# v projected ahead of w_conf_out, and triangular levels that keep only X^T: a hybrid conformer / gated-delta / MoE step on one core

## The reference, cut to what matters

```
p   = rmsnorm(h) @ w_in                              # u pair, q, k, v, z, a, b, two gates
c   = silu(layernorm(dwconv31(u)));  y_a = c @ w_conf_out + b_conf_out
qkv = silu(dwconv4(p[q, k, v]));  q, k = l2norm(q), l2norm(k)
a_mat = I + strict_lower(beta k k^T * decay)         # per head and chunk
u, w  = solve(a_mat, [beta v, beta k exp(gc)])       # triangular solve
v_new = u - w S;  o = q_dec S + (q k^T * decay) v_new;  S = S exp(gl) + k_dec^T v_new
h  += (sig(gA) * y_a + sig(gB) * (norm(o) * silu(z)) @ w_dn_out) @ w_out
h  += moe_top4_of_32(rmsnorm(h));   y = rmsnorm(h)
```

## Time and profile before

| what | value |
|---|---|
| median of 3 runs | 1618.7 us (1615.04 to 1619.51) |
| profiled execution | 1620.38 us, span 1618.5 us, mean granted TensorE clock 0.92 |
| busy over the span | PE 81%, PEld 44%, DVE 34%, POOL 14%, ACT 12% |
| HBM traffic | 480.5 MB, mean 297 GB/s |

### The profile page before, as it was taken

One profiled execution on the slowest core, in us unless ns is written; L12 is line 12 of the kernel. 1 busy time (PEld: TensorE's weight loads), 2 busy tenths in 40 slices (PEclk: granted clock), 3 DMA queues, 4 the chain that ended last, 5 costly groups with the idle time before them and its releaser, 6 DMA issues.

```text
span 1618.5 us, 31060 instructions
## 1 busy us (share of the span) xinstructions
PE 1317.7 (81%) x11104; PEld 711.4 (44%) x11105; DVE 542.4 (34%) x1370; ACT 202.0 (12%) x524; POOL 225.8 (14%) x350
## 2 busy tenths in 40 slices
PE   4899999988878987866999896966696987866955
PEld 4677777757867642322343332322232332222312
DVE  2799846175366234101211111111021121101254
ACT  2211232322122020000000000000000000000001
POOL 2006600207131001000100000000010000001310
PEclk9999999998989988887999998988898998888987
DMA  7766545304005678999997999999999999999996
GB/s 140 241 159 119 123 107 154 104 6 114 2 1 178 217 265 350 418 418 416 420 418 289 355 417 419 419 416 420 419 416 420 419 392 391 420 418 418 417 403 240
DMA packets 184543, 480.50 MB, mean 297 GB/s; under 512 B 15932, under 2 KB 113468, under 8 KB 151659
## 3 DMA queue, kind: packets, MB, share of 16 engines
q1 hardware_dynamic: 172909, 463.37, 76.0%
q0 software_dynamic: 2560, 10.29, 1.6%
q10 hardware_dynamic: 9024, 6.17, 1.2%
HBM read 462.42 MB, written 18.21 MB: 297 GB/s over the span
## 4 chain that ended last, share of the span: by engine, by line
PE 61%; DMA 18%; DVE 8%; SPq 6%; issue 4%; ACT 2%; POOL 1%; DVEq 0%; POOLq 0%; ACTq 0%
PE bank L1226 18%; DMA arena<-in_w_up 16%; PE bank L776 15%; PE bank L1238 11%; PE bank L1194 4%; PE bank L1212 3%; SPq L374 2%; PE bank L1118 2%; PE bank L1126 2%; DMA arena<-in_w_in 2%; SPq L442 2%; ACT gate L1621 1%; DVE arena L1955 1%; DVE gate L2226 1%; PE bank L1037 1%
## 5 line engine op out<-in xcount | busy, mean ns | idle before, releaser
L1226 PE MATMUL bank<-arena,gate 128*32 128x512 f32 x3264 | 415.8, 640 | 134.5 <-DMA arena<-in_w_up 134.5
L1226 PEld LDWEIGHTS bank<-arena,gate 128*32 128x32 f32 x3264 | 103.6, 113 | 404.5 <-issue 275.5
L776 PE MATMUL bank<-arena 128*128 128x304 f32 (+1 forms) x1024 | 261.3, 418 | 5.8 <-DMA arena<-in_w_in 4.7
L2241 DVE COPY gate<-bank 128x256 f32<-128x256 f32 x46 | 19.5, 425 | 637.1 <-PE bank L1238 637.1
L776 PEld LDWEIGHTS bank<-arena 128*128 128x128 f32 x1024 | 196.3, 192 | 69.5 <-issue 7.3
L1238 PE MATMUL bank<-arena,gate 128*32 128x256 f32 x3264 | 189.3, 384 | 29.4 <-ACT gate L1621 29.4
L1238 PEld LDWEIGHTS bank<-arena,gate 128*32 128x32 f32 x3264 | 112.5, 111 | 93.9 <-issue 26.6
L1744 DVE SCALAR_TENSOR_TENSOR acc<-arena,pcol,acc x240 | 126.4, 607 | 0.1
L675 POOL TENSOR_TENSOR qkv<-qkv 128x192 f32<-128x192 f32 x46 | 29.3, 638 | 617.7 <-DVE qkv L2185 617.7
L1212 PE MATMUL bank<-qkv 128*128 128x512 f32 x102 | 62.2, 694 | 49.6 <-DVE gate L2227 22.5
L1194 PE MATMUL bank<-qkv 128*32 128x256 f32 (+1 forms) x1224 | 87.8, 403 | 0.7 <-DVE qkv L2149 0.7
(11 more groups left out here) (411 smaller groups left out, 1202.8 us busy)
## 6 DMA issues: line engine op xcount, KB each, us to landing
arena<-in_w_up SPq DMA_DIRECT2D x256, 1024.0 KB, 12.5
arena<-in_w_down SPq DMA_DIRECT2D x256, 512.0 KB, 8.8
arena<-in_w_in SPq DMA_DIRECT2D x64, 512.0 KB, 11.9
y_d<-gate ACTq DMA_DIRECT2D x188, 32.0 KB, 4.9
y_d<-zs POOLq DMA_DIRECT2D x1, 4608.0 KB, 22.2
arena<-in_w_conf_out SPq DMA_DIRECT2D x8, 512.0 KB, 4.9
arena<-in_state_dn_S SPq DMA_DIRECT2D x8, 512.0 KB, 7.2
arena<-in_w_dn_out SPq DMA_DIRECT2D x1, 4096.0 KB, 13.9
```

Source lines behind the costliest of these rows:

```text
L776: last = mm(bank[2 * (j % 2) + f][:, 0:cols.stop - cols.start], wring[:, j, k, P * f:P * (f + 1)], rhs[:, k, cols], start=(k == 0), stop=( ...
L1226: last = mm(hidden(q)[v], xgT[:, i, SL * q0:SL * (q0 + 1)], parts(wup[k], q)[v], start=False, stop=(k == KC - 1), skip_group_check=True)
```

## The change

- v is round 7, and TensorE's l2 sums stand behind its steps. w_conf_out is loaded as round 8 and is applied in eight halves of 128 output columns (`conf_half`, one bank), placed by hand between the setup steps of chunk 0; VectorE evacuates each (`conf_evac`).
- The conf tails are transposed and stored before rounds 5 and 6. The q/k/v tails are turned by plain matmuls with the identity into four 32-partition strips of two banks, copied by two instructions and stored by 12 transfers.
- In a level the two products become one: X^T is kept, X is made of it by transposes and a copy on ScalarE. The last level updates X. X is not built in the setup.
- The constants of the packed work are made before the squares of q and k; token masks, sums, products, start and packed levels move to earlier levels; sample products go to levels 4, 5, 6 and behind k times S.
- Buffers are moved so that the lifetimes allow it: the sample states take the slots of the weight ring (their load waits for the last conf half), `w_out` the chunk buffers (its load waits for `s_done`), the experts' slots follow.

```diff
@@ sync
-            win_group(7, 0, a["w_conf_out"][0].rearrange("(k p) n -> p k n", p=P))
-            win_group(8, 4 * D)
...
+            sp.wait_ge(s["tail_evac"], 2)
             sp.dma_start(a["cp"][0, 0], uout[0:CH, :]).then_inc(s["tail_out"], 16)
...
+            win_group(7, 4 * D)
+            win_group(8, 0, a["w_conf_out"][0].rearrange("(k p) n -> p k n", p=P))
+
+            sp.wait_ge(s["tail_evac"], 4)
+            for b, q in ((0, 0), (0, 1), (0, 2), (0, 3), (1, 0), (1, 1)):
+                cols = slice(2048 * b + 512 * q, 2048 * b + 512 * (q + 1))
+                sp.dma_start(a["dp"][0, 0][:, cols], qout[32 * q:32 * q + SH, b, :]).then_inc(s["qkv_tail_out"], 16)
...
+            sp.wait_ge(s["job_done"], 13 + KC)
             for h in range(H):
                 sp.dma_start(s0[:, h, :, :], a["state_dn_S"][0, :, h].rearrange("n k v -> k n v")
@@ tensor
+            pe.wait_ge(s["ab_ready"], 1)
+            for g in range(2):
+                for k in range(4 * g, 4 * g + 4):
+                    last = nc.tensor.transpose(bank[6 + g][0:62, P * (k % 4):P * (k % 4 + 1)], utail[:, k, :], ident[:])
+                last.then_inc(s["tail_t_done"], 1)
             with pe.Fori(5, 7) as it:
                 win_round(it)
...
+                pe.wait_ge(s["win_bank_free"], 7 * WRING + (j + 1))
+                win_step(7, j, xnT)
+                l2_sums(j)
+
+            def turn_tails():
+
+                pe.wait_ge(s["win_bank_free"], 34)
+                for k in range(24):
+                    b, r = divmod(k, 16)
+                    q, i = divmod(r, 4)
+                    last = mm(bank[5 + b][32 * q:32 * (q + 1), P * i:P * (i + 1)], qtail[:, k, :], ident[:], start=True, stop=True,
+                              skip_group_check=True)
...
+            def conf_half(m):
+
+                j, f = divmod(m, 2)
+                if f == 0:
+                    pe.wait_ge(win_in[j], 8 * 32 + 32)
+                if m:
+                    pe.wait_ge(s["conf_mm_evac"], m)
...
+                for k in range(KC):
+                    last = mm(bank[7][:, 0:N2], wring[:, j, k, P * f:P * (f + 1)], acc[:, k, TS],
+                              start=(k == 0), stop=(k == KC - 1))
+                last.then_inc(s["job_done"], 1)
@@ tensor, chunk 0 setup (rows, then)
+                    conf_half(0)
+                    turn_tails()
+                    conf_half(1)
+                    packed_sums()
+                    conf_half(2)
+                    pe.wait_ge(s["packed_dve"], DVE_STEP["sums"])
+                    pe.wait_ge(s["tail_evac"], 4)
+                    pe.wait_ge(s["l2_scaled"], 16)
... (products k k^T, k q^T)
+                    conf_half(3)
+                    conf_half(4)
... (transposes of k and v)
+                    conf_half(5)
... (transposes of um)
+                    conf_half(6)
+                    packed_rows()
+                    conf_half(7)
@@ tensor, a level
                         for h in range(4 * g, 4 * g + 4):
+                            last = nc.tensor.transpose(bank[2 + g][:, P * (h % 4):P * (h % 4 + 1)], xt[:, h, :], ident[:])
+                        last.then_inc(s["xt_turned"], 1)
+                        for h in range(4 * g, 4 * g + 4):
                             last = mm(bank[g][:, P * (h % 4):P * (h % 4 + 1)], um[:, h, :], xt[:, h, :],
...
+                            left, right = (x, zt) if lev < LEVELS - 1 else (zt, x)
+                            last = mm(bank[g][:, P * (h % 4):P * (h % 4 + 1)], left[:, h, :], right[:, h, :],
                                       start=True, stop=True)
-                        if lev < LEVELS - 1:
-                            for h in range(4 * g, 4 * g + 4):
-                                last = mm(bank[g][:, P * (h % 4):P * (h % 4 + 1)], x[:, h, :], zt[:, h, :],
-                                          start=True, stop=True)
@@ tensor, chunk 0, behind a level's product
+                        if lev == 1:
+                            packed_products()
+                        elif lev == 2:
                             packed_turn()
-                        elif lev == 6:
...
+                        elif lev < 6:
+                            packed_v(lev - 2)
+                            if lev > 3:
+                                sample_products(kmask, "kmask", 0, lev - 4)
+                        else:
+                            meta_state()
                             sample_products(qmask, "qmask", 256, 0)
@@ scalar, a level
+                        act.wait_ge(s["xt_turned"], lev * 2 + (12 * c + g - 1))
+                        fn(heads(u_x, P)[:, 4 * g:4 * g + 4, :], bank[2 + g][:, :].rearrange("p (h n) -> p h n", h=4), ACT.Copy
+                           ).then_inc(s["zt_copied"], 1)
@@ vector, chunk 0 setup
+                    conf_evac(0)
+                    tails_out()
+                    conf_evac(1)
+                    packed_sums()
+                    l2_scale(1)
+                    l2_scale(0)
+                    conf_evac(2)
+                    dve.wait_ge(s["l2_scaled"], 16)
...
-                dve.wait_ge(s["um_ready"], 7 * c + 1)
-                v.tensor_tensor(x, eye.to_broadcast((P, H, P)), um, ALU.subtract)
@@ vector, a level
-                        last = v.tensor_tensor(x[:, hs, :], x[:, hs, :], four(bank[2 + g]), ALU.subtract)
-                        if lev < LEVELS - 1:
-                            last = v.tensor_tensor(xt[:, hs, :], xt[:, hs, :], four(bank[g]), ALU.subtract)
-                        last.then_inc(s["x_updated"], 1)
+                        w = xt if lev < LEVELS - 1 else x
+                        v.tensor_tensor(w[:, hs, :], w[:, hs, :], four(bank[g]), ALU.subtract).then_inc(s["x_updated"], 1)
@@ gpsimd, chunk 0
+                if c == 0:
+                    pool.wait_ge(s["qkv_tail_out"], 16 * 12)
+                    token_masks(kmask, k_p[:, 1:3, :].rearrange("p g n -> p (g n)"), H)
...
                         if lev == 1:
-                            packed_constants()
+                            token_masks(qmask[:, 0:4], q_p[:, 0, :], 4)
...
+                            packed_level(0)
                         elif lev == 3:
-                            packed_sums()
...
+                            token_masks(qmask[:, 4:8], q_p[:, 1, :], 4)
+                            packed_level(1)
+                        elif lev < 6:
+                            packed_level(lev - 2)
```

More of the change, by code:

```diff
@@ L66 @@
 WRING = 4
-STEPS = 9 * WRING
 A_UH = WRING * 2048
@@ L86, in steps @@
     return {name: i + 1 for i, name in enumerate(names.split())}
[L89 removed]
+PE_STEP = steps("spread sums rows u qk ktr vtr umtr zt1 v1 zt2 v2 zt3 v3 ks vnm sm qs vns os ot")
 DVE_STEP = steps("gb sums dt_arg dt uu qk kd x0 x1 x2 x3 vmm s r o scaled out")
 ACT_STEP = steps("packed exps dt vb zt1 zt2 zt3 oq vns root")
[L92 removed]
+POOL_STEP = steps("const um kmask qmask0 um0 qmask um1 um2 um3 vm0 vm1")
 def first(b):
@@ L867, in packed_sums, with packed_rows @@
                 packed(mm(bank[4][:, 68:70], same_s, gb_p[:, 0, 1:3], start=True, stop=True))
+            def packed_rows():
                 pe.wait_ge(s["packed_pool"], POOL_STEP["um"])
-                packed(mm(bank[5][:, 0:384], ones[:], um_p, start=True, stop=True))
+                pe.wait_ge(s["uq_evac"], 8)
+                packed(mm(bank[6][:, 0:384], ones[:], um_p, start=True, stop=True))
             def packed_products():
-                pe.wait_ge(s["packed_dve"], DVE_STEP["sums"])
+                pe.wait_ge(s["packed_dve"], DVE_STEP["dt_arg"])
                 pe.wait_ge(s["packed_act"], ACT_STEP["exps"])
+                pe.wait_ge(s["conf_mm_evac"], KC)
                 for i in range(3):
@@ L925, in meta_state @@
                     rows = slice(32 * r, 32 * (r + 1))
-                    last = mm(bank[2 + r][:, 0:2 * P], kd_p[rows, 0, :], vmeta[rows, :, :], start=True, stop=True)
+                    last = mm(meta_bank[r][:, 0:2 * P], kd_p[rows, 0, :], vmeta[rows, :, :], start=True, stop=True)
                 packed(last)
@@ L1793, in _ @@
             stt(g_t, g_t, -1.0, alog.unsqueeze(1).to_broadcast((P, 3, H)), ALU.mult, ALU.mult).then_inc(s["rates_ready"], 1)
+            for g in range(2):
+                dve.wait_ge(s["tail_t_done"], g + 1)
+                v.tensor_copy(uout[:, 512 * g:512 * (g + 1)], bank[6 + g][0:62, :]).then_inc(s["tail_evac"], 1)
             QLINKS = 2 + 4 * (SW - 1)
```

348 lines of the change are left out of this document (159 added, 189 removed).

## The result

The changed kernel takes 1593.45 us (median of 4 runs, 1589.45 to 1597.06) against 1617.39 us for the kernel before (4 runs, 1615.04 to 1619.51): a ratio of 0.984, 95% interval 0.9816 to 0.9864, or 23.9 us less. The prediction was 1594 us, faster. The profiled execution took 1589.45 us with a span of 1587.7 us, 30.8 us less than the span in the earlier trace rows.

A forecast was written before the change was run, and what follows sets the result against it. The prediction took the mixer before the last projection to set the total one for one, with DMA full afterwards. 7.1 + 13.4 + 5.5 - 1.2 = 24.8 us off 1618.7 gave 1594 us, range 1586 to 1606.

The forecast's parts named there:

- What bounds the kernel: Stage of experts: full DMA engines set the end, so mixer gains before the last projection (525.19 us) count one for one.
- The state load: Before chunk 0's level 4: load waits for the last conf half, lands at 390 us, needed at 397, 7 us slack.
- Projections and setup: From the v projection to chunk 0's level 1: conf matmuls cover the setup, level 1 starts at 371 us, 7 us earlier.
- the tails: Chunk 0 setup: 24 conv tails as plain matmuls, two passes each, taken at 5.3 us, lower bound 1.5.
- The rival in which the setup serialises: Chunk 0 setup: VectorE's queue holds the conf bank at most halves; 5 to 8 us lost, about 1601 us; chance 0.15.
- The cover: Chunk 0 setup: 32 us of conf matmuls hide the setup's waits; if it fails, each wait returns by itself.
- Chunk 0: Levels of the first chunk to the matmul with vb: 46.3 us instead of 59.7, a gain of 13.4 us.
- Level 1's new wait: Chunk 0, after level 1: packed products wait 2.4 us for the exponential of decay rows, behind VectorE's own update.
- The 1.2 us for hand-overs: All levels: 0.1 us a level set against the gain for hand-overs not drawn, 1.2 us in all.
- Chunk 1: Second chunk: fewer subtractions, levels 3 to 5 at a 5.7 us pitch, shorter level 6 and residual; 5.5 us gained.
- The rival on the other side: Levels: transposes do not keep TensorE's full clock; 1655 us if cold in both chunks, 1619 in chunk 1 alone; chance 0.06.
- Copies and mask as the chain: Levels: ScalarE's copies and the late mask set 6.0 us a level; 8 us of gain lost, about 1602 us; chance 0.12.

The follow-up runs named there:

- the kernel run again: The changed kernel, unaltered, measured a second time against the kernel before: 1593.98 us against 1621.4, ratio 0.9839 (0.9822 to 0.9857).
- the halves in one piece: Changed kernel with all eight conf halves ahead of the first chunk's setup, two banks in turn: 1607.99 us, ratio 0.9914 to the kernel before.
- the stream of transposes: Changed kernel with 300 added 128x128 transposes in one stream ahead of the first projection: 1628.26 us, one run.
- the turn with two passes: Changed kernel with the levels' transposes replaced by plain matmuls with the identity, two passes instead of one: 1608.98 us, one run.
- the roots later: Changed kernel with four small reorderings, plus chunk 1's output roots on ScalarE in level 2 instead of 1: 1588.5 us, ratio 0.979 to before.
- the filler of transposes: 34 unread transposes in the wait before chunk 1's level 1: 1583.77 us on the changed kernel; 1580.14 us with reordering and later output roots.

## Why the prediction was right, point by point

- **What bounds the kernel.** Shown. The last projection moved by 29.4 us and the span by 30.8; in the kernel run again by 26.9 and 26.3. What the mixer gains comes out of the total, within the scatter of the stage of experts.
- **The state load.** It had to be there for the first sample product and was, with 8 to 10 us to spare (7 predicted).
- **Projections and setup, 7.1 us.** 10.25 in the profile. Sums were done at 319.3 and not 320.3, which is within the scatter of this point. From there to level 1, 48.6 us were measured and 50.7 predicted (320.3 to 371). The largest miss is the tails, 3.3 us and not 5.3, between the bounds of 1.5 and 5.3 that I had set. The wait for the scalings came as 1.79 us (2.1 predicted), that between halves 3 and 4 as 0.70 (0.7), that before half 7 not at all (0.4), nor did the late start of the first half (0.5). The halves took 0.8 us more than the 31.0, and that cancels most of these. The rival in which the setup serialises did not come: only one half had to wait.
- **The cover.** That it pays is shown by the halves in one piece; how much of their 14.2 us is the cover is not, since VectorE's order there adds to the waits. My price for its loss was too low, since I counted waits and not the clock that goes with them (4.3 us).
- **Chunk 0, 13.4 us.** 13.2. Levels 8.5, 5.3, 7.4, 7.1, 6.9, 11.2 against 8.7, 5.2, 7.0, 7.1, 7.0, 11.3. Level 3 is the one that was drawn short: its packed Z waits 1.09 us for a packed mask behind the token mask. Level 1's new wait was 2.0 us, not 2.4. The 1.2 us for hand-overs that I had not drawn were not needed: level by level the drawing was 0.2 us short. The pad and the high price of the tails thus erred the same way.
- **Chunk 1, 5.5 us.** 5.9, but made up otherwise. Levels 1 and 2 gave 2.3 us (1.0 predicted), levels 3 to 5 3.7 (3.0), level 6 with the residual 1.2 (1.1): 7.2 in all. Of this, 1.5 us are the clock behind the output's turn: it was 0.66 there before (481 to 486 us) and 1.00 now. Before, then after:

```profile
481.70 1.95 PE L968 MATMUL bank<-ident,qkv 128*128 128x128 f32 x8 [0.94 <-DVE qkv L1965]
483.44 2.78 PE L1029 MATMUL bank<-arena,temps 128*128 128x128 f32 x16
```

```profile
458.09 1.09 PE L978 MATMUL bank<-ident,qkv 128*128 128x128 f32 x8 [0.94 <-DVE qkv L2007]
```

The setup of chunk 1 took 1.3 us more and not 0.4 less. The 0.4 us came (the wait before level 1 is 4.05 us instead of 4.40), but the row sums ran at a granted clock of 0.57 (3.68 instead of 1.98 us). The prediction had neither of these two changes of the clock. They are of nearly the same size and of opposite sign, so that 5.9 beside 5.5 is partly luck.
- **The clock.** The rival on the other side is refuted by the levels themselves (1.00 from 361 to 423 us in this profile, with one stretch of 0.57 in that of the kernel run again) and by the stream of transposes.
- **Copies and mask as the chain.** They did not set the pace, but for a wait of 0.79 us for ScalarE's copies in level 2 of chunk 1: levels 4 and 5 of chunk 0 were no longer than drawn, and in chunk 1 TensorE had 17.00 us of 17. What paces a level now is TensorE; the turn with two passes shows it, as the added passes come through in ten levels of twelve.
- **The total.** 7.1 + 13.4 + 5.5 - 1.2 = 24.8 us predicted. Measured 23.9 by the runs of the first comparison, 26.1 by those of the second (23.2 to 28.9 from the ratio's interval), and 29.4 by the one profile. The 4.6 us between 24.8 and the profile's 29.4 are the earlier end of the sums (1.0), the tails (2.0), the pad (1.2), chunk 1 (0.4), small change in the setup and behind the levels (0.2), less chunk 0 (0.2). Nearly all the terms that were off erred to one side, and the runs stand below what the profiles show: they lie as close to the forecast as they do partly by chance.

## What to carry to other kernels

Price a turn by its passes: with one pass for each head it was cheaper to turn X^T than to keep X beside it. With two passes it gained only 4.2 of the 15.2 us (187.7 against 191.9 us), of which 1.7 were luck with the clock. Fill waits of TensorE with work that has to be done anyway; it saves the wait and also the slower passes behind it, here 4.3 us on 9.9. Where no such work is at hand, passes that nobody reads save the slower passes, though not the wait: 34 of them in a wait of 4 us made the level behind it 1.8 us shorter. And after a reordering look at which wait is next before counting the gain: moving the output roots took away a wait of 0.8 us and moved two others from level 2 to level 3, where slow passes behind them took the gain back.

## What was not expected of the hardware

- Transposes held the full clock by themselves for 33 us, at 0.110 us a pass, and in the same execution nothing but transposes had run when the pace rose from 0.21 to 0.11 us a pass.
- A short pause can cost the clock or not: after the same 2.0 us of idling the granted clock was 1.00 in one execution of the changed kernel and 0.57 in another. At the start of chunk 1, four passes of 512 columns took 1.98 us in the kernel before and in four of the changed ones (with the roots later, with the plain turns, with the filler of transposes in either kernel), but 3.25 to 3.78 us in eight others, the kernel after twice among them, always after the same wait of 0.82 us. What decides it stays open.
- Passes into a strip of 32 columns: 48 took 3.39 us (0.071 us each) with neighbours in the same strip and 1.94 us (0.040) with neighbours in different ones. Even in the same strip they cost less than a pass of the full width, 0.111 us.
